# A two-block network on one core: the first feed forward's first matrix by seven block products, and a new order in the S5 scan

## The reference, cut to what matters

```python
for layer in range(2):
    ...
    h = _rmsnorm(x, norm_g[layer, 0]) * (1.0 + scale_m) + shift_m
    mix = _mixer_conv_retention(h, ...) if layer == 0 else _mixer_s5(h, ...)
    x = x + gate_m * mix
    h = _rmsnorm(x, norm_g[layer, 1]) * (1.0 + scale_f) + shift_f
    x = x + gate_f * (jnp.square(jax.nn.relu(h @ w_fc1[layer])) @ w_fc2[layer])   # 1024 -> 4096 -> 1024
```

## Time and profile before

| | us |
|---|---|
| median of the runs | 3493.67 |
| profiled execution | 3498.12 |
| its span, first to last instruction | 3496.3 |
| first matrix of the first feed forward | 2357.9 to 2577.3 |
| its second matrix | 2577.3 to 2802.0 |
| S5 stage up to the gated unit | 2807 to 2972 |

### The profile page before, as it was taken

The page is one execution under the profiler, slowest core; times in us unless marked ns, Lnnn a source line. Parts: engine busy times, 40 slices in busy tenths (PEclk is TensorE's granted clock), DMA queues, the critical chain, the costliest instruction groups (busy, mean ns, idle before and its releaser), DMA issues. The chain is left out here.

```text
span 3496.3 us, 29943 instructions
## 1 busy us (share of the span) xinstructions
PE 3148.9 (90%) x10952; PEld 1680.0 (48%) x10952; DVE 1999.0 (57%) x4319; ACT 734.3 (21%) x1623; POOL 659.3 (19%) x649
## 2 busy tenths in 40 slices
PE   8999799988898878877878889999999978999998
PEld 3453454433333333333333434534444457778887
DVE  5555742676776677776676319435663367455423
ACT  2133211222222222222221220112110033121000
POOL 0110100244443444444444100000000000000000
PEclk9999899999999998998898999999999999999999
DMA  5743411699999999999999422113444344212222
GB/s 190 248 151 122 157 50 71 255 421 421 421 421 422 421 417 414 415 421 412 414 421 414 199 103 85 48 35 119 162 178 151 122 174 169 97 61 85 86 88 80
DMA packets 118675, 799.16 MB, mean 229 GB/s; under 512 B 13728, under 2 KB 16416, under 8 KB 31872
## 3 DMA queue, kind: packets, MB, share of 16 engines
q0 software_dynamic: 91312, 619.09, 44.0%
q1 hardware_dynamic: 27216, 178.15, 14.3%
HBM read 767.83 MB, written 29.36 MB: 228 GB/s over the span
## 5 line engine op out<-in xcount | busy, mean ns | idle before, releaser
L1315 PE MATMUL po<-pair,diag 128*128 128x512 f32 x2048 | 991.1, 641 | 197.7 <-ACT diag L1398 197.3
L1492 DVE SCALAR_TENSOR_TENSOR pair<-pair,h_tm 128x1024 f32<-128x1024 f32 x512 | 619.1, 1225 | 323.7 <-DMA pair<-in_peer_uv,idx 316.9
L1315 PEld LDWEIGHTS po<-pair,diag 128*128 128x128 f32 x2048 | 410.3, 205 | 751.5 <-issue 484.3
L1208 POOL DMA_INDIRECT pair<-in_peer_uv,idx x512 | 586.9, 1146 | 939.2 <-PE po L1315 658.2
L1391 ACT ACTIVATE ge<-a 128x2 f32<-128x2 f32 (+2 forms) x178 | 36.4, 204 | 930.8 <-DVE pair L1492 930.8
L1642 PE MATMUL acc<-a,ring 128*128 128x512 f32 x512 | 220.9, 592 | 0.0
L1627 PE MATMUL acc<-hT,ring 128*128 128x512 f32 x480 | 206.2, 592 | 0.0
L1398 ACT ACTIVATE diag<-ident,wt 128x128 f32<-128x128 f32 x512 | 169.1, 392 | 41.0 <-DVE wt L1496 40.5
L1642 PEld LDWEIGHTS acc<-a,ring 128*128 128x128 f32 x512 | 97.3, 190 | 122.5 <-issue 122.5
L1627 PEld LDWEIGHTS acc<-hT,ring 128*128 128x128 f32 x480 | 91.2, 190 | 114.8 <-issue 114.8
L523 PE MATMUL acc<-hT,first 128*128 128x512 f32 x304 | 136.0, 602 | 5.4 <-ACT mg L707 5.4
(11 more groups left out here) (471 smaller groups left out, 4111.7 us busy)
## 6 DMA issues: line engine op xcount, KB each, us to landing
ring<-in_w_fc SPq DMA_DIRECT2D x62, 1024.0 KB, 4.8
mg<-in_ada_w POOLq DMA_DIRECT2D x96, 512.0 KB, 4.9
s_tables<-table POOLq DMA_DIRECT2D x16, 1664.0 KB, 6.6
tab<-s_tables SPq DMA_DIRECT2D x16, 1664.0 KB, 6.4
ring<-in_w SPq DMA_DIRECT2D x15, 1024.0 KB, 4.8
first<-in_w_first SPq DMA_DIRECT2D x14, 1024.0 KB, 5.2
other<-in_w_first SPq DMA_DIRECT2D x14, 1024.0 KB, 5.0
pair<-in_peer_uv,idx POOLq DMA_INDIRECT x512, 15.7
```

Of the source, the lines that this page charges most:

```text
L1208: pool.indirect_dma_start(out=pair[:, at, :], out_offset=None, in_=core.dram["peer_uv"][:, :], in_offset=bass.IndirectOffsetOnAxis(ap=idx[ ...
L1315: last = pe.matmul(po[:, t % 2, half * 512:(half + 1) * 512], diag[:, at, :], pair[:, at, D + half * 512:D + (half + 1) * 512], start=firs ...
L1492: dve.scalar_tensor_tensor(row, row, 1.0, h_tm[:, t, :], ALU.mult, ALU.mult, accum_out=a[:, s:s + 1]).then_inc(dotted, 1)
```

## The change

`feed_forward` is replaced by `feed_forward_first`, which takes the first matrix by `Pairs`. The squares are merged with the Relu on VectorE. `vector_powers` is cut into five parts, behind pairs 0, 1, 3, 5 and 7; all sixteen table rounds stand in the second matrix, two for each output block, ahead of its add. One of the table buffers now lies in the memory of the weight sums, and two others in that of the token sums. The weights of the first matrix are laid out by halves. In `s5` the order of TensorE's and ScalarE's lists changes.

```diff
+def feed_forward_first(core, layer, following, beside):
...
+        scalar_at, vector_at = [0, 2, 2, 4, 6], [0, 1, 3, 5, 7]
...
+        @block.tensor
+        def _(pe):
+            feed.chunk(pe, 0, True)
+            pairs.first(pe, products.ready)
+            for p in range(1, HT):
+                pairs.tensor(pe, p)
+            for j in range(KT):
+                if j >= 3:
+                    pe.wait_ge(added, j - 2)
...
+                        if j == 0 and half == 0:
+                            pe.wait_ge(squared, f + 1)
...
+        @block.scalar
+        def _(act):
+            products.scalar(act)
+            for p in range(HT):
+                if p:
+                    pairs.copies(act, p)
+                    pairs.first_quarter(act, p, a[:, p, LOW]).then_inc(pairs.c_taken, 1)
...
+                for i in range(5):
+                    if scalar_at[i] == p:
+                        scalar_powers(act, i)
+            for j in range(KT):
+                scalar_round(act, 2 * j)
+                scalar_round(act, 2 * j + 1)
...
+                act.wait_ge(added, j + 1)
+                sums.square(act, j)
...
+        @block.vector
+        def _(dve):
...
+            for p in range(HT):
+                if p:
+                    if p + 1 < HT:
+                        pairs.halves.add(dve, p + 1)
+                    pairs.quarters(dve, step, p, a[:, p, HIGH], a[:, HT + p, LOW], a[:, HT + p, HIGH])
+                    dve.wait_ge(pairs.c_taken, p)
...
+                step.mark(dve.scalar_tensor_tensor(a[:, p, :], a[:, p, :], 0.0, a[:, p, :], ALU.max, ALU.mult))
+                dve.scalar_tensor_tensor(a[:, HT + p, :], a[:, HT + p, :], 0.0, a[:, HT + p, :], ALU.max, ALU.mult).then_inc(squared, 1)
+                for i in range(5):
+                    if vector_at[i] == p:
+                        vector_powers(dve, i)
+            for j in range(KT):
+                vector_round(dve, 2 * j)
+                vector_round(dve, 2 * j + 1)
+                dve.wait_ge(made, HT + 2 * j + 2)
...
-    table = st.sb("table", [P, 2, N_TABLE])
+    table = [place, st.sb("table", [P, N_TABLE])[:, :]]
...
```

In the S5 stage, TensorE's list (`outputs` is cut in two, its first part without the states' products) and ScalarE's:

```diff
-            turn(0)
-            own(0)
             for n in range(8):
                 kk, part = divmod(n, 2)
...
                 last.then_inc(put, 1)
+            turn(0)
+            own(0)
...
                     turn(i + 1)
                     own(i + 1)
+                if i:
+                    outputs_own(i - 1)
+                if i + 1 < ROUNDS:
                     toeplitz(i + 1, 0)
                 if i:
-                    outputs(i - 1)
+                    outputs_states(i - 1)
...
-            ends_weights(0)
-            own_taps(0)
             products.scalar(act)
             for n in range(8):
...
+            ends_weights(0)
+            own_taps(0)
```

More of the change, by code:

```diff
@@ L1581, in gate_col @@
     return 3 * KT * which + 2 * KT
[L1584 to L1687, removed]
@@ L1975, in _ @@
                 dve.scalar_tensor_tensor(core.xT[:, 4 + j, :], flat(1), gate(4 + j), core.xT[:, 4 + j, :], ALU.mult, ALU.add).then_inc(added, 1)
+def feed_forward_first(core, layer, following, beside):
+    N1, HT = FF // P, FF // P // 2
+    with Stage(core) as st:
+        a = st.sb("a", [P, N1, S])
+        th = st.sb("token_sums", [P, 3, KT // 2, S // 2])
+        u, v = st.sb("parts_x", [P, S // 2]), st.sb("parts_y", [P, S // 2])
+        bank = st.ps("bank", [P, 4, S])
+        acc = st.ps("acc", [P, 3, S])
+        products = modulated(core, st, 2 * layer + 1)
+        sq = th[:, :, :, :].rearrange("p i k s -> p (i k s)")[:, 0:2 * S].rearrange("p (b s) -> p b s", b=2)
+        sums = Sums(core, st, st.ps("ms", [P, S])[:, :], sq=sq)
+        made, squared, added, v_step = (st.sem(n) for n in ("made", "squared", "added", "v_step"))
+        chunks = [block_of(core, f"w_fc1_{layer}", i) for i in range(HT)] + [block_of(core, f"w_fc2_{layer}", i) for i in range(2 * KT)]
+        feed = Feed(core, st, made, [n + 1 for n in range(len(chunks))], chunks, following)
+        pairs = Pairs(core, st, feed, made, bank, core.hT, th, u[:, :], v[:, :])
+        pool, scalar_powers, scalar_round, vector_powers, vector_round = beside(
+            core, st, pairs.halves.sums[:, :, :, :].rearrange("p b i x -> p (b i x)")[:, 0:N_TABLE],
+            th[:, :, :, :].rearrange("p i k s -> p (i k s)")[:, 2 * S:])
+        block = st.block()
+        block.gpsimd(pool)
+        scalar_at, vector_at = [0, 2, 2, 4, 6], [0, 1, 3, 5, 7]
+        @block.sync
+        def _(sp):
+            feed.load(sp)
+        @block.tensor
[7 more added lines that the diff above has]
+                    pe.wait_ge(added, j - 2)
+                for half in range(2):
+                    w = feed.chunk(pe, HT + 2 * j + half, True)
+                    for k in range(16):
+                        f = half * 16 + k
+                        if j == 0 and half == 0:
+                            pe.wait_ge(squared, f + 1)
+                        last = pe.matmul(acc[:, j % 3, :], w[:, k * P:(k + 1) * P], a[:, f, :], start=(f == 0), stop=(f == N1 - 1))
+                    last.then_inc(made, 1)
+                if j >= 1:
+                    sums.add(pe, j - 1)
+            sums.add(pe, KT - 1)
+        @block.scalar
[5 more added lines that the diff above has]
+                    pairs.first_quarter(act, p, a[:, p, LOW]).then_inc(pairs.c_taken, 1)
+                else:
+                    act.wait_ge(pairs.x_made, 1)
+                    act.activation(a[:, 0, :], pairs.x(0), ACT.Copy).then_inc(pairs.x_copied, 1)
+                    act.wait_ge(made, 1)
+                    act.activation(a[:, HT, :], pairs.y(0), ACT.Copy).then_inc(pairs.y_copied, 1)
+                for i in range(5):
[4 more added lines that the diff above has]
+                scalar_round(act, 2 * j + 1)
+                if j == KT - 1:
+                    act.preload_act_table_set(LN_EXP)
+                act.wait_ge(added, j + 1)
+                sums.square(act, j)
+            sums.root(act)
+        @block.vector
+        def _(dve):
+            step = Steps(dve, v_step)
+            products.vector(dve)
+            pairs.halves.add(dve, 1)
+            dve.wait_ge(products.ready, KT)
+            pairs.token_sums(dve)
+            for p in range(HT):
[4 more added lines that the diff above has]
+                    dve.wait_ge(pairs.c_taken, p)
+                else:
+                    dve.wait_ge(pairs.x_copied, 1)
+                    dve.wait_ge(pairs.y_copied, 1)
+                step.mark(dve.scalar_tensor_tensor(a[:, p, :], a[:, p, :], 0.0, a[:, p, :], ALU.max, ALU.mult))
[7 more added lines that the diff above has]
+                dve.wait_ge(made, HT + 2 * j + 2)
+                x = core.xT[:, j, :]
+                at = gate_col(2 * layer + 1) + j
+                dve.scalar_tensor_tensor(x, acc[:, j % 3, :], core.mod[:, at:at + 1], x, ALU.mult, ALU.add).then_inc(added, 1)
@@ L2388, with s5_tables @@
 N_TABLE = 3328
-def s5_tables(core, st):
+def s5_tables(core, st, place, part):
     N = SG
@@ L2406, in s5_tables @@
     ang, turns = st.sb("ang", [P, 4, SN]), st.sb("turns", [P, 4, SN])
-    part = st.sb("part", [P, 4, 4, ST, SC])
-    table = st.sb("table", [P, 2, N_TABLE])
+    part = part.rearrange("p (n g t c) -> p n g t c", n=4, g=4, t=ST)
+    table = [place, st.sb("table", [P, N_TABLE])[:, :]]
     k_landed, v_step, ready, done, tabled, a_step, sined, prepared = (st.sem(n) for n in (
@@ L2416, in piece @@
         at, n = TABLE[name]
-        return table[:, r % 2, at:at + n]
+        return table[r % 2][:, at:at + n]
     def pool(eng):
@@ L2428, in pool @@
             eng.wait_ge(sined, r + 1)
-            eng.dma_start(core.scratch[r * P:(r + 1) * P, :], table[:, r % 2, :]).then_inc(written[r % 2], 16)
+            eng.dma_start(core.scratch[r * P:(r + 1) * P, :], table[r % 2]).then_inc(written[r % 2], 16)
             if r + 2 < ROUNDS:
@@ L2466, in s5_tables, with vector_powers, angles_and_size, first_angles @@
     step_of = []
-    def vector_powers(dve):
-        step = Steps(dve, v_step)
-        step_of.append(step)
+    def vector_powers(dve, part):
+        if part == 0:
+            step_of.append(Steps(dve, v_step))
+        step = step_of[0]
         TTm = lambda out, a, b, op=ALU.mult: step(dve.tensor_tensor(out, a, b, op))
-        step(dve.tensor_scalar(lr[:, :], core.col("s5_lr"), -1e-4, None, ALU.min))
+        many = lambda x: x[:, :].unsqueeze(2).to_broadcast([P, N, ST])
+        def angles_and_size(i):
+            TTm(mag[:, :, :], k[:, i, :, :], many(ld))
+            TTm(s[:, :, :], k[:, i, :, :], many(th))
+            reduced(dve, step, s[:, :, :], spare[:, :, :])
+            angles(dve, step, s[:, :, :], c[:, :, :])
+            dve.tensor_copy(spare[:, :, :], c[:, :, :]).then_inc(ready, 1)
+            dve.wait_ge(ready, 3 + i)
+        if part == 0:
```

(27 more changed lines are left out.)

11 lines of the change are left out of this document (7 added, 4 removed).

## The result

The changed kernel takes 3464.3 us (median of four runs, 3461.6 to 3466.8) where the kernel before takes 3494.7 beside it: 30.4 us less, a ratio of 0.9907 with a 95% interval of 0.9894 to 0.9919. The prediction said 3462.0 and 31.7 us. The profiled executions are 3498.12 and 3464.62 us; their spans differ by 33.4 us, and 4.2 of that lie ahead of the first feed forward, where nothing was changed.

A forecast was written before the change was run, and what follows sets the result against it. TensorE, busy 90% of the span, was taken to bound the kernel. Gains of 17.1 (first matrix), 6.3 (start of S5) and 8.3 us (scan) sum to 31.7, from the median 3493.7 to 3462.0 us; range 3450 to 3477.

The forecast's parts named there:

- First matrix, TensorE's side: First feed forward, first matrix: pairs after the first take 12.08 us in place of 13.71, saving 24.5 us.
- Two waits behind parts two and three: First matrix: long parts of the powers delay weight sums TensorE needs, stalls of 2.85 and 3.0 us, 5.9 together.
- Clock behind them: First matrix: the two stalls may halve TensorE's clock, 1.5 us lost for both, bounds 0 and 4.
- Second matrix: First feed forward, second matrix: all sixteen table rounds fit beside TensorE's work with 6 us spare a block; cost zero.
- the rival: Second matrix: table rounds become the bound; if each waits in full for its write, 66 us lost, 3528; chance 0.04.
- End of the stage: End of second matrix: the last table write lands with 2.5 us to spare before the stage ends; cost zero.
- Start of the S5 stage: S5 start: tokens turned ahead of the first table, 6.3 us gained; 8.3 or 2 depending on when the clock rises.
- Scan: Scan rounds: the output's own part runs inside the wait for taps, 14 x 0.59 = 8.3 us gained, 0.28 wait left.
- The sum: Whole kernel: 17.1 + 6.3 + 8.3 = 31.7 us gained, 3462.0 us from the median; chance of 3456 to 3468: 0.59.
- The rule of the Trainium skill: Table writes in second matrix: VectorE's two-port operations lock out GpSimd, 3.1 us instead of 0.62 per DMA; under 1 us lost.

The follow-up runs named there:

- experiments 1: The changed kernel with both long parts of the powers cut at their middle, seven parts in place of five: 3454.96 us.
- 7: The changed kernel with the powers cut into seven parts and only one clearing of semaphores allowed in the program: 3456.08 us.
- 9: Repeat, on the same chip as the changed kernel's rerun, of the kernel with cut powers and only one clearing of semaphores: 3455.16 us.
- experiment 2: The changed kernel with the first table's turning, own products and copies back ahead of the tokens in the S5 stage: 3472.58 us.
- 3: The changed kernel with the output's own part back behind the turning of the taps in the scan: 3472.16 us.
- 8: The changed kernel run once more, unchanged: 3467.34 us, ratio to the kernel before 0.9904 to 0.9931.
- experiment 5: The changed kernel with three products of each table round made once more, so rounds take 12.98 us: 3469.27 us.
- experiment 6: The changed kernel with each table round waiting for the write of the round before, not of two rounds before: 3527.31 us.

## Why the prediction was right, step by step

- **First matrix, TensorE's side** (24.5 us): shown. 12.08 us a pair, and 24.7 us gained in experiments 1, 7 and 9, where no wait is left (219.81 - 195.11).
- **Two waits behind parts two and three** (2.85 and 3.0 us): shown; TensorE's late starts are 2.79 and 2.96 us against 12.08 us pairs, in pairs 5 and 7, in each of the six profiles with these parts, and gone once the parts are cut.
- **Clock behind them** (1.5 us): measured 1.9 in the changed kernel. The first pair's 1.7 us at the lower clock was not in the sum; it is not the change's, since experiments 2, 3 and 8, whose first matrix is the same, have it at 202.7 to 202.8 us. That is 17.1 us gained, as forecast; the changed kernel's own profile shows 15.35.
- **Second matrix** (0): shown, and the place where it would fail lies beyond 13 us a round (experiment 5) and costs about what the rival said (experiment 6: 59 us in the second matrix and its end, against 66).
- **End of the stage** (2.5 us to spare): the step that was mis-sized. GpSimd's drain of 3.0 us behind the landing was left out. In the changed kernel the last write is issued at 2777.28 and lands 5.6 us later, and the drain ends at 2786.17, where the stage could end at 2787.20: 1.0 us to spare. It cost nothing here, but had the last two rounds together been 1.1 us longer, it would have shown (in experiment 5 they are 4.4 us longer, and the stage ends 3.4 us late).
- **Start of the S5 stage** (6.3 us): 7.6 measured, 7.6 taken back by experiment 2. The clock came back about when the forecast said, behind groups three and four, but these groups took 1.7 to 1.8 us each at the lower level, not 2.1 (half of the first two groups' 4.17 in the earlier trace rows, which are slower here too, 4.35), and the other four 4.2 us, not 4.7: the turning ended 14.4 us behind the first shift, not 15.6. In the other executions with the new order this stretch was 14.75 to 16.57 us.
- **Scan** (8.3 us): 8.2, with 0.29 us of wait left, as said.
- **The meeting of all engines** that moved ahead of the gated unit was not foreseen; it cost 1.05 us of idle there and gave 1.1 back at the second feed forward. The clock took 1.6 more in the first pair there, as it did in four of the seven profiles with this meeting.
- **The sum**: 31.7 us forecast, 30.4 by the medians, 29.2 by stretch. The terms were off by 1.75 (first matrix), -1.3 (start of the S5 stage), 0.1 (scan) and 2.0 us (behind the scan), which partly cancel, and medians move by some 3 us: that the total lies so close is in part luck. The mechanisms were as said.
- The rule of the Trainium skill ("SBUF — State Buffer", Who interferes with whom) that VectorE's two-port operations lock GpSimd out: no run here shows it, and the prediction applied it too widely, since the same section says that `tensor_tensor`, most of a round's work, has no such mode. With rounds back to back all sixteen issues took 0.54 to 0.55 us, as before.

## What to carry to other kernels

When work of another stage is laid beside a paced one, its deadline counts, not its sum: here 7.1 us in one piece cost nothing and 12.75 did, though VectorE had some 6 us to spare in every pair. The limit between them, 9.9 us (13.8 - 2.45 - 1.45), is an estimate that no run tried. Work out for each piece from when to when it may stand, and cut it there. An in-order engine's short operation behind a long wait (ScalarE's shifts behind the first table) is worth looking for at every stage's start. And compare such changes by stretches between the same instructions, since gains of 3 us vanish in a median.

## What had not been expected of the hardware

- GpSimd's drain at the end of the stage in which it wrote the tables takes 3.0 us (2997 ns in all eleven profiles), where the other engines' take 0.6 to 1.2 there. In experiment 5 the next stage began 3.5 us after the last landing. Why the drain takes so long isn't settled: at two other stages' ends of the changed kernel GpSimd's longest takes 9.2 and 19.7 us, at the rest under 0.3 us.
- The same wait of 2.64 us brought the granted clock down to 0.50 in six profiles of six (16 records in 5.32 to 5.41 us in place of 3.62), and the wait of 2.79 us, two pairs later, in two of six (6.69 and 6.78 us). The 2.49 us ahead of the gated unit did it in four of seven. What makes the first fall each time and the others not isn't settled by these runs.
